# Six plain groups ahead of the 14 seven-product groups and two behind, GpSimd in the scaling of x, snapshots ahead of weight splits

## What is computed

```python
def swiglu(x, w_gate, w_up, w_down):
    return (jax.nn.silu(x @ w_gate) * (x @ w_up)) @ w_down

# per layer, D_FF = 2816
f = swiglu(rms_norm(h, nw[0]), ffn_w_gate[layer, 0], ffn_w_up[layer, 0], ffn_w_down[layer, 0])
h = h + 0.5 * rms_norm(f, nw[1])
...
f = swiglu(rms_norm(h, nw[4]), ffn_w_gate[layer, 1], ffn_w_up[layer, 1], ffn_w_down[layer, 1])
h = h + 0.5 * rms_norm(f, nw[5])
```

## Time and profile before

| | |
|---|---|
| time, median of 3 runs | 2159.97 us (2156.52 to 2160.62) |
| the profiled execution: its own time, its span | 2162.67 us, 2160.9 us |
| TensorE matmul busy | 2083.1 us, 96% |
| VectorE, ScalarE, GpSimd busy | 1303.0 (60%), 965.6 (45%), 99.9 us (5%) |
| granted TensorE clock, mean | 0.99 |

### The profile page before, as it was taken

One profiled execution on the slowest core, in us unless ns is written; L12 is line 12 of the kernel. 1 busy time (PEld: TensorE's weight loads), 2 busy tenths in 40 slices (PEclk: granted clock), 3 DMA queues, 4 the chain that ended last, 5 costly groups with the idle time before them and its releaser, 6 DMA issues.

```text
span 2160.9 us, 38367 instructions
## 1 busy us (share of the span) xinstructions
PE 2083.1 (96%) x16054; PEld 1984.5 (92%) x16054; DVE 1303.0 (60%) x1886; ACT 965.6 (45%) x1627; POOL 99.9 (5%) x97
## 2 busy tenths in 40 slices
PE   8899999999999989999999899999999998999998
PEld 7899999998999989999999899999998797999887
DVE  6988522567485498864228887521763449887423
ACT  4555422436435545554224555422453554555312
POOL 0000000100051200000000000000000020000000
PEclk9999999999999999999999999999999999999999
DMA  4333432331110223333312233432332122333332
...
DMA packets 329041, 180.63 MB, mean 84 GB/s; under 512 B 15849, under 2 KB 323344, under 8 KB 328878
## 3 DMA queue, kind: packets, MB, share of 16 engines
...
q0 software_dynamic: 1024, 2.86, 0.5%
...
q10 hardware_dynamic: 334, 0.14, 0.0%
...
## 4 chain that ended last, share of the span: by engine, by line
PE 84%; DVE 10%; ACT 3%; issue 2%; DMA 1%; POOL 0%; DVEq 0%; SPq 0%; ACTq 0%
PE psum L701 36%; PE psum L1239 23%; PE psum L713 10%; PE psum L927 6%; DMA stage<-ffn_w_gate 1%; DVE w_hl L565 1%; DVE scaled_x L1900 1%; PE psum L3015 1%; DVE t_both L1999 1%; ACT w_hl L1500 1%; DVE ring_raw L1866 1%; DVE seven_x L1944 1%; DVE ring_raw L1864 1%; PE psum L3074 1%; DVE w_hl L1846 1%
## 5 line engine op out<-in xcount | busy, mean ns | idle before, releaser
L701 PE MATMUL psum<-x_hl,w_hl 128*128 128x264 f32 (+1 forms) x4080 | 554.2, 296 | 7.7 <-DVE w_hl L565 4.2
L701 PEld LDWEIGHTS psum<-x_hl,w_hl 128*128 128x128 f32 x4080 | 524.6, 190 | 30.3 <-DVE w_hl L565 9.8
L565 DVE TENSOR_TENSOR w_hl<-stage,w_hl 128x1024 fp32r<-128x1024 f32 (+1 forms) x198 | 260.0, 1313 | 366.4 <-ACT w_hl L558 366.4
L1239 PE MATMUL psum<-seven_x,w_hl 128*128 128x264 f32 (+1 forms) x2688 | 346.2, 284 | 14.8 <-ACT t_both L1616 4.9
L1239 PEld LDWEIGHTS psum<-seven_x,w_hl 128*128 128x128 f32 x2688 | 330.3, 188 | 25.5 <-issue 25.5
L558 ACT ACTIVATE w_hl<-stage 128x1024 fp32r<-128x1024 f32 (+1 forms) x198 | 222.6, 1125 | 259.8 <-PE psum L701 110.7
L1239 PE MATMUL psum<-x_hl,w_hl 128*128 128x264 f32 (+1 forms) x2016 | 269.4, 288 | 28.1 <-DVE x_hl L1944 28.1
L701 PE MATMUL psum<-acts,w_hl 128*128 128x264 f32 x2376 | 288.9, 284 | 0.0
L701 PEld LDWEIGHTS psum<-acts,w_hl 128*128 128x128 f32 x2376 | 288.6, 188 | 0.0
L1239 PEld LDWEIGHTS psum<-x_hl,w_hl 128*128 128x128 f32 x2016 | 258.4, 193 | 28.8 <-issue 28.8
L713 PE MATMUL psum<-x_hl,w_hl 128*128 128x264 f32 (+1 forms) x1728 | 220.3, 286 | 4.9 <-DVE w_hl L565 4.7
...
## 6 DMA issues: line engine op xcount, KB each, us to landing
...
```

What stands on the lines that cost most here:

```text
L565: dve.tensor_tensor(weights(core.w_hl[:, slot.ring, 1, :], *kind), weights(core.stage[:, slot.stage, :], *kind), weights(core.w_hl[:, slot ...
L701: op = pe.matmul(out, lhs, moving[:, moved, kt, t0:t0 + n], start=first and part + moved == 0, stop=last and part == 1)
L1239: op = pe.matmul(k.psum[:, bank, 0:w], k.w_hl[:, slot.ring, side, at:at + P], moving(moved, kt), start=start and kt + side + moved == 0, s ...
```

## The change

It does the following:

- Groups 0 to 5 are plain, 6 to 19 of seven products, 20 and 21 plain. Group 5 is done by halves.
- Of `scaled_x`, VectorE makes tiles 0 to 3 as before. ScalarE multiplies tiles 4 to 7 by the norm weight (at slot 0) and GpSimd multiplies them by `rinv`. GpSimd also makes S_M7 and S_M3; VectorE keeps S_M5 and S_M6.
- The tables spread the quarters over slots 5 to 14, in the order of need, and TensorE waits for each quarter where it uses it.
- The weight split of slot 5 moves from slot 2 to slot 1 in the programs of ScalarE and VectorE.
- The snapshot of stage r = 2 stands ahead of that stage's weight split, and in the last seven-product group so do those of r = 1.
- `acts` tiles 0 to 5 are split during the seven-product groups 7 to 13, and tiles 6 to 20 in equal shares (4, 4, 4, 3) in groups 20 and 21; on ScalarE ahead of the silu there.

```diff
-SEVEN_FROM, SEVEN = 4, 14
-KEPT_FROM = SEVEN_FROM
+SEVEN_FROM, SEVEN = 6, 14
+EARLY_KEPT = 6
...
+X_ORDER = (S_M6, S_M5, S_M7, S_M3, 4 + A11, 4 + A12, 4 + A22, 4 + A21)
+
+
+def x_count(phase, q):
+
+    return phase.x0 + X_ORDER.index(q) + 1
...
-    pe.wait_ge(k.x_lo, phase.x0 + 4 + A11 + 1)
+    pe.wait_ge(k.x_lo, x_count(phase, 4 + A11))
...
     pe.wait_ge(k.w_lo, slots[1].count())
+    pe.wait_ge(k.x_lo, x_count(phase, S_M6))
     pe.wait_ge(k.product_kept, 4 * j + 1)
...
+def early_tile(n):
+
+
+    t = n - SEVEN_FROM - 1
+    return t if 0 <= t < EARLY_KEPT else None
...
-X_HIGH_AT = {4: (0, 1), 5: (2, 3), 6: (4, 5), 7: (6, 7)}
+X_HIGH_AT = {5: (S_M6, S_M5), 7: (S_M7, S_M3), 9: (4 + A11, 4 + A12), 11: (4 + A22,), 13: (4 + A21,)}
+
+
+def weighted_tiles(core, act, phase):
...
+    for kt in range(DT // 2, DT):
+        col = phase.before.pre_col + kt
+        op = act.activation(k.scaled_x[:, kt, t0:TOK], k.h[:, kt, t0:TOK], ACT.Copy, scale=k.norm_cols[:, col:col + 1])
+    op.then_inc(k.x_summed, 1)
...
             s = slot.local
+            kept_first = is_seven(n) and (r == 2 or r == 1 and not is_seven(n + 1))
+            if kept_first:
+                seven_kept(k, act, phase, n, r)
             if s == 0:
                 groups_ahead_hi(k, act, phase, 1)
-            elif s > 1:
+            elif s == 1:
+                groups_ahead_hi(k, act, phase, 2)
+            elif s > 2:
                 groups_ahead_hi(k, act, phase, s)
             if is_seven(n):
-                seven_kept(k, act, phase, n, r)
+                if not kept_first:
+                    seven_kept(k, act, phase, n, r)
+                if r == 3 and early_tile(n) is not None:
+                    act_high(k, act, phase, early_tile(n))
...
     if q == S_M6:
+        dve.wait_ge(k.x_summed, sums_before(phase) + SUMS)
...
-TILES_AT = {1: range(0, DT // 2), 2: range(DT // 2, DT)}
-SUMS_AT = {3: (S_M5, S_M6), 4: (S_M7, S_M3)}
-X_LOW_AT = {4: (0, 1), 5: (2, 3), 6: (4, 5), 7: (6, 7)}
+TILES_AT, SUMS_AT = 1, 4
+X_LOW_AT = {6: (S_M6, S_M5), 8: (S_M7, S_M3), 9: (4 + A11, 4 + A12), 11: (4 + A22,), 14: (4 + A21,)}
...
+                if r == 1 and early_tile(n - 1) is not None:
+                    act_low(k, dve, phase, early_tile(n - 1))
...
+def gpsimd_groups(core, pool, phase):
+
+
+    k, t0 = core, parts(phase.cols)[0][0]
+    pool.wait_ge(k.x_summed, sums_before(phase) + 1 + DT // 2)
+    for kt in range(DT // 2, DT):
+        tile = k.scaled_x[:, kt, t0:TOK]
+        pool.tensor_tensor(tile, tile, k.rinv[:, t0:TOK], ALU.mult).then_inc(k.x_summed, 1)
+    quarter_sums(core, pool, phase, S_M7)
+    quarter_sums(core, pool, phase, S_M3)
```

More of the change, by code:

```diff
@@ L1260, in seven_products @@
     pe.wait_ge(k.w_lo, slots[3].count())
+    pe.wait_ge(k.x_lo, x_count(phase, S_M3))
     pe.wait_ge(k.product_kept, 4 * j + 4)
@@ L1516, in kept_tiles @@
 def kept_tiles(n, side):
-    last = SEVEN_FROM + SEVEN
-    first = KEPT_FROM
-    step = 2 * (n - last) + side
-    shares = [3] * 4 + [2] * 2 + [1] * (2 * (FT - last) - 6)
-    at = first + sum(shares[0:step])
-    return range(at, min(at + shares[step], FT - 1 if step < len(shares) - 1 else FT - 1))
+    step, steps = 2 * (n - SEVEN_FROM - SEVEN) + side, 2 * (FT - SEVEN_FROM - SEVEN)
+    share = -(-(FT - 1 - EARLY_KEPT) // steps)
+    first = EARLY_KEPT + share * step
+    return range(first, min(first + share, FT - 1))
+def early_tile(n):
+    t = n - SEVEN_FROM - 1
+    return t if 0 <= t < EARLY_KEPT else None
 def group_buffers(core, n):
@@ L1556, in x_high @@
         cols = slice(half[part][0], half[part][0] + w)
-        act.wait_ge(k.x_summed, q0 + DT)
+        act.wait_ge(k.x_summed, q0 + 1 + DT)
         if part:
@@ L1589, in scalar_groups @@
             else:
+                if n > SEVEN_FROM:
+                    for t in kept_tiles(n, 0):
+                        act_high(k, act, phase, t)
                 cols = token_cols(gate[:, :], phase.cols)
@@ L1597, in scalar_groups @@
                     act.activation(cols, bank_cols(k, slot.pair, phase.cols), ACT.Silu).then_inc(k.gate_silu, 1)
-                    for t in kept_tiles(n, 0):
-                        act_high(k, act, phase, t)
+            if s == 0:
+                weighted_tiles(k, act, phase)
             for q in X_HIGH_AT.get(s, ()):
@@ L1890, in act_low, with scaled_tiles @@
                       token_cols(k.acts[:, 0, t, :], phase.cols).bitcast(F32), ALU.subtract).then_inc(k.act_lo, 1)
-def scaled_tiles(core, dve, phase, tiles):
+def scaled_tiles(core, dve, phase):
     k = core
     t0 = parts(phase.cols)[0][0]
-    for kt in tiles:
+    for kt in range(DT // 2):
         col = phase.before.pre_col + kt
@@ L1901, in scaled_tiles, with quarter_sums @@
                                  k.rinv[:, t0:TOK], ALU.mult, ALU.mult).then_inc(k.x_summed, 1)
-def quarter_sums(core, dve, phase, which):
+def quarter_sums(core, engine, phase, which):
     k = core
@@ L1933, in x_low @@
     w = half[0][1]
-    dve.wait_ge(k.x_hi, phase.x0 + q + 1)
+    dve.wait_ge(k.x_hi, x_count(phase, q))
     if q < 4:
@@ L1965, in vector_groups @@
                 seven_outputs(k, dve, phase, n, r)
-                continue
-            if n < SEVEN_FROM:
-                plain_outputs(k, dve, phase, n, r, slot)
-            elif r:
-                plain_product(k, dve, phase, n, slot)
-            if s == 0:
-                groups_ahead_lo(k, dve, phase, 1)
-            elif s > 1:
-                ahead, role = group_at(s + AHEAD) if s + AHEAD < phase.slots else (0, 0)
-                if is_seven(ahead) and role == 1:
-                    weight_sums(k, dve, phase, ahead)
-                groups_ahead_lo(k, dve, phase, s)
-            if n < SEVEN_FROM and r:
-                act_low(k, dve, phase, n)
-            if n >= SEVEN_FROM:
-                for t in kept_tiles(n, r):
-                    act_low(k, dve, phase, t)
-            if s in TILES_AT:
-                scaled_tiles(k, dve, phase, TILES_AT[s])
-            for which in SUMS_AT.get(s, ()):
-                quarter_sums(k, dve, phase, which)
+                if r == 1 and early_tile(n - 1) is not None:
+                    act_low(k, dve, phase, early_tile(n - 1))
+            else:
+                if n < SEVEN_FROM:
+                    plain_outputs(k, dve, phase, n, r, slot)
+                elif r:
+                    plain_product(k, dve, phase, n, slot)
+                if s == 0:
+                    groups_ahead_lo(k, dve, phase, 1)
+                elif s == 1:
+                    groups_ahead_lo(k, dve, phase, 2)
+                elif s > 2:
+                    groups_ahead_lo(k, dve, phase, s)
+                if n > SEVEN_FROM:
+                    for t in kept_tiles(n, r):
+                        act_low(k, dve, phase, t)
+            if s + AHEAD == group_slot(SEVEN_FROM):
+                weight_sums(k, dve, phase, SEVEN_FROM)
+            if s == TILES_AT:
+                scaled_tiles(k, dve, phase)
+            if s == SUMS_AT:
+                quarter_sums(k, dve, phase, S_M5)
+                quarter_sums(k, dve, phase, S_M6)
             for q in X_LOW_AT.get(s, ()):
@@ L1998, in plain_outputs @@
     dve.wait_ge(k.slot_used, slot.count())
+    if n and not r:
+        dve.wait_ge(k.act_full, phase.a0 + n)
     dve.tensor_tensor(up if r else gate, src, rinv, ALU.mult).then_inc(k.scaled, 1)
@@ L2190, in gpsimd_program @@
                 gpsimd_split(k, pool, step)
+        elif kind == "dense" and step.kind == "gu":
+            gpsimd_groups(k, pool, step)
         elif kind == "dense" and step.kind == "rows":
```

34 lines of the change are left out of this document (19 added, 15 removed).

## The result

The changed kernel took 2087.07 us (median of 4 runs, 2085.12 to 2090.2) against 2160.15 for the kernel before: ratio 0.9667, 95% interval 0.965 to 0.9683. The forecast was 2090. The profiled execution of the changed kernel took 2086.23 us, with a span of 2084.5.

The account below looks back on a forecast made before the run. TensorE was taken to bound the kernel, losing time to waits and slow clock in the gate/up phases. 72 us won, less 0.5 a phase kept back, gave 70 and a median of 2090 us (range 2084 to 2097, chance 0.62).

Parts of the forecast that it names:

- Entry and plain groups: Ahead of and into the seven-product groups: 10.1 us a phase won at the entry, 1.2 in plain groups, 0.5 before the window.
- Seven-product groups and way out: Earlier snapshots close thirteen gaps of 0.35 us, 4.6 us a phase, and a 1.0 us wait on leaving the groups.
- Sum: Four gate/up phases: 70.3 us in the windows and 2 ahead of them, 72; 70 after keeping back 0.5 a phase.
- VectorE slows too: On the way in, contention beside GpSimd costs VectorE 4 us, within 9 free, so nothing; ends 0 and 11.5.
- my sum: VectorE's work up to the entry: 40.2 us in a stretch of 49.2, so 9 us free.
- GpSimd's chain: GpSimd's tiles and sums before the entry: tiles of 1.44 to 2.11 us, sums of 2.9 to 4.2, done before they are due.
- The rule of the Trainium skill: GpSimd contends with VectorE instructions having two SBUF inputs and is about half as fast; cited as speaking against GpSimd's share.
- The period: Rival: seven-product groups stay at 10.53 us because something other than the snapshot's place sets them; 2108 us, chance 0.14.
- GpSimd did take from VectorE: Rival: contention makes VectorE enter the seven-product groups 2.5 us late and the clock falls; 2112 us, chance 0.11.
- `x_hl`'s turning over: Rival: A11 and A12 still come late at the entry, whatever VectorE's load; 2114 us, chance 0.06.
- GpSimd holding up the plain groups: Rival: GpSimd's chain is late and TensorE stands 22 us a phase in the plain groups; 2178 us, chance 0.03.
- the second rival: GpSimd takes from VectorE on the way in, 11.5 us at worst; 2112 us, chance 0.11.

Follow-up runs that it names:

- e2_snap_only: The kernel before with only the snapshots of r = 2, and of r = 1 in the last seven-product group, ahead of the weight splits: 2134.89 us.
- e10_gpsimd_spent: The changed kernel with VectorE making all tiles and sums, plus eight GpSimd products a phase that nothing reads: 2091.27 us, ratio 0.9679 to the kernel before.
- e7_share_only: The kernel before with only the GpSimd and ScalarE share of the tiles and sums added: 2169.61 us, ratio 1.0052 to the kernel before.
- e3_vector_all: The changed kernel without the GpSimd and ScalarE share, VectorE making all scaled tiles and block sums: 2085.03 us, ratio 0.9658 to the kernel before.

## Why the prediction was right, and what was mis-sized

- **Entry and plain groups (11.8 us a phase).** Right. On the way in TensorE waits for nothing but the output ahead of the phase, at clock 1.00. From `e2_snap_only` to the changed kernel, all but the snapshots, the runs give 2134.89 - 2087.07 = 47.8 us, 4 x 11.8 = 47.
- **Seven-product groups and way out (4.6 + 1.0).** Right in kind and in the count of thirteen gaps, low in size. Behind the first 24 matmuls the groups are 5.8, 5.9, 6.0 and 7.0 us shorter in the four phases, against 5.6 each. The fourth, with its matmuls of 256 columns, I had not worked out: a group takes 9.93 us there for 10.36, so a gap is 0.43 us, and the wait at the way out was 1.12.
- **Sum.** Over the stretch of each phase the traces give 17.90, 17.95, 18.10 and 18.70 us, 72.65 in all, against 72 in the working; the fourth, taken as 17.6 + 0.5, is the one that is over. The stretch runs from the start of group 2 to the end of the last plain group, and new waits, 1.0 us in all, are already taken off. I had taken 2 us off the 72 for them. That is why the time came out at 2087 and not 2090.
- **VectorE slows too.** The mis-sized term: I took 4 us, from half of GpSimd's time at most; it was 6.8, out of 11.9 us of GpSimd's work. The tightest point was not where I had looked (slots 8 and 10). It was slot 6, whose split ended at 767.6 as TensorE wanted it at 767.55; in the fourth phase it cost a wait of 0.24 us. `e10_gpsimd_spent` (a slot later) and `e7_share_only` show the waits when such a margin is gone. With VectorE busy 43.82 of 49.54 us, 5.7 us stayed free, near the 9 - 4 = 5 of my sum. That is luck: without the contention VectorE's work is 43.82 - 6.8 = 37.0 us (`e3_vector_all` gives 42.12 - 5.2 = 36.9) and not the 40.2 of my sum, which took 18 outputs where 16 fall in the stretch and added up durations that overlap in the trace by up to 0.08 us. The two errors, 2.8 us too little and 3.2 too much, nearly cancel.
- **GpSimd's chain.** Tiles 1.66 us each, sums 2.48 and 2.81: within or below my bounds of 1.44 to 2.11 and 2.9 to 4.2. VectorE never stood still for it.
- **The rule of the Trainium skill.** The Trainium skill, "GPSIMD Engine Reference", section Key points, has GpSimd contend with VectorE instructions that have two SBUF inputs. The traces agree, since just these grew (a split from 1.22 to as much as 3.48 us), and those with an input in PSUM kept their 0.7. It gives no size for it.
- **Rivals.** The period did not stay; late snapshots bring it back, so VectorE's order was not behind it. GpSimd did take from VectorE, 6.9 us with its work spent for nothing, but not up to a wait at the entry. `x_hl`'s turning over was in time. GpSimd holding up the plain groups did not happen: at the old place of the groups the kernel is 10 us slower, but by the lengthened splits of the second rival, and VectorE waits for no result of GpSimd.
